# Three bank pairs in the up phases and a rearranged first up phase of a two-block fp32r transformer kernel

## The chip, the cores and the metric

The kernel runs on one core of one Trainium2 chip. The metric is the device time of one execution in microseconds (us); lower is better. PE is TensorE (PEld its weight loads), DVE is VectorE, ACT is ScalarE, POOL is GpSimd, and SP is SyncE, which issues most transfers. The text calls a matmul instruction a product.

## The reference

The input x has 256 rows of width 1024. Two transformer blocks follow each other. Cut to what matters here:

```python
# block 1
x = x + _moba(_rmsnorm(x, norm_mix), moba_w_qkv, moba_w_o)
u = _causal_dwconv(_rmsnorm(x, norm_ffn) @ w_up, conv_w, conv_b)   # D_FF = 2816, 3 taps
gate, up = jnp.split(u, 2, axis=-1)
x = x + (jax.nn.silu(gate) * up) @ w_down
x = _rmsnorm(x, norm_final)
# block 2: mod = silu(c) @ w_mod + b_mod gives shifts, scales and gates
x = x + 0.5 * (1 + ga1) * swiglu(modulate(rms_norm(x, g_ffn1), sh1, sc1), w1_gate, w1_up, w1_down)
x = x + (1 + ga2) * hybrid_mixer(modulate(rms_norm(x, g_mix), sh2, sc2), w_in, b_f, g_q, g_k, w_o)
x = x + 0.5 * (1 + ga3) * swiglu(modulate(rms_norm(x, g_ffn2), sh3, sc3), w2_gate, w2_up, w2_down)
```

All weights are float32.

## The kernel before

**Numbers in two parts.** Every weight and every activation that PE multiplies is split into a high part (rounded to fp32r, written by ACT) and a low part (the rest, a subtraction on DVE). One product of the reference is then three on PE: high by high (L1305), high weight by low activation (L1306), low weight by high activation (L1307).

**Slabs and chunks.** The weights come as slabs of 256 columns by up to 8 k-tiles (1 MB). SP loads slab i into one of three buffers `raw`; for each pair of k-tiles (a chunk) ACT writes `whi` (L688) and DVE writes `wlo` (L931), each in one of three buffers. The load of slab i + 3 waits for the last `wlo` of slab i.

**Phases.** Ten phases follow each other: qkv1, o1, up1, down1, up2, down2, qkv3, o3, up4, down4. up1 is the convolved FFN of block 1; up2 and up4 are the two gated ones of block 2. An up phase has 22 slabs and 22 groups, gate and up columns in turn; a group is the 256 output columns that PE accumulates in two banks of PSUM before somebody takes them out (evicts them). A slab of an up phase is 8 k-tiles x 2 halves x 3 = 48 products. A down phase has 4 groups of three slabs each (8, 8 and 6 k-tiles). The groups are numbered through the program: up1 has 16 to 37, down1 38 to 41, up2 42 to 63, down2 64 to 67, up4 85 to 106, down4 107 to 110.

**Banks.** Group g uses banks 2*(g%2) and 2*(g%2)+1, so two pairs in turn (`at`, L531 to L533). Before its first product PE waits until group g - 2 is evicted (`emptied(need, g - 2)`, L1296). Banks 4 (norm sums), 6 (transposes) and 7 are kept for other work; 4, 5, 1 and 3 also hold attention scores.

**Evictions.** In up1 (tags `cg`, `cu`) ACT scales the group and adds the bias into `ca` (L808), DVE adds the two other taps straight from the banks (L1079, four instructions; the last one frees the banks), then ACT applies silu for a gate group (L814), and for an up group DVE multiplies (L1091), ACT writes `Hhi` (L842, L847) and DVE `Hlo` (L1175). In up2 and up4 ACT's silu reads the gate group (L822) and DVE's multiplication the up group (L1113). The first groups of up2 and up4 take their norm afterwards and need more DVE work (L1103 to L1130).

**Order.** `Plan.lay` writes one list of steps, and each engine runs its own steps of it in that order: a step that waits holds up all later ones of its engine. `evict` puts weight conversions between the parts of an eviction. `MOD_STEPS` says at which slab a step `mod` is put: one dot product of `w_mod` on DVE (L1020), 72 in all. At the end of o1 the steps are the norm of up1 (PE sums the squares, L1318 and L1322; ACT takes the root, L745 and L748), then for each of 8 tiles `latey` (DVE L971 into `yb`, ACT L766 into the high part of `A`) and `latelo` (DVE L978, the low part). ACT needs one table of functions for ln and exp and another for silu; `silu()` loads the second (L673) and `exp_ln()` the first (L667).

**Resets.** At the start of some slabs (`RESETS`) PE issues one tiny product on constants (L1299), which in this trace also marks where a slab begins.

Of the kernel before, what the change touches and what calls it, by code (L numbers as in the profile page):

```python
# [14 lines left out]
P = 128  # L15
S = 256
# [4 lines left out]
C = 256  # L21
# [16 lines left out]
RAW_OF = {"up2": 0, "qkv3": 1, "up4": 2}  # L38
LATE_OF = {"up1": 0, "up2": 1, "qkv3": 2, "up4": 3}
S_BANKS = (4, 5, 1, 3)  # L40
HALVES = ("qkv1", "o1", "qkv3", "o3")
NORM_BANK, T_BANK, O_BANK = 4, 6, 7
O_BANKS = {2 * C: S_BANKS[0], 3 * C: S_BANKS[1]}
NORM_OF = {"qkv1": 0, "up1": 1, "up2": 2, "qkv3": 3, "up4": 4}
# [4 lines left out]
def slab_table(a):  # L49
# [38 lines left out]

RESETS = {"up1": (1, 6, 12, 18), "down1": (0,), "up2": (1, 4, 6, 14), "down2": (0,), "up4": (1, 4, 6, 14), "down4": (0,)}
MOD_STEPS = {  # L90
    "qkv1": lambda i: int(i > 2) + int(i in (4, 7, 10)), "o1": lambda i: int(i < 15), "up1": lambda i: int(i in (29, 33)),
    "down1": lambda i: int(i < 50), "up2": lambda i: int(i >= 55) * (1 + int(i % 4 == 3)), "down2": lambda i: int(i < 83),
    "qkv3": lambda i: int(i in (89, 91, 93, 95)), "o3": lambda i: 0, "up4": lambda i: int(i > 106) * int(i % 2 == 0), "down4": lambda i: 0}
QKV3_TILE = {0: 0, 512: 8, 1024: 16, 1536: 4, 2048: 12, 2560: 20}

# [21 lines left out]
class Plan:  # L117
# [13 lines left out]
    def lay(self):  # L131
        slabs, st = self.slabs, self.st
# [118 lines left out]
        norm = "qkv1"  # L251
# [46 lines left out]
        for i, (ph, tag, c0, k0, nk, last, width, _) in enumerate(slabs):  # L298
# [11 lines left out]
            g = o_group + c0 // C if tag == "o" else group  # L310
            if tag == "ot":
                g = o_group + 2
# [7 lines left out]
            for kt in range(nk):  # L320
                kg = k0 + (kt // 3 if tag == "ot" else kt)
# [53 lines left out]
            if i + 1 < len(slabs) and slabs[i + 1][0] != ph and ph in NEXT_NORM:  # L375
                norm = NEXT_NORM[ph]
                if norm == "up1":
                    st.put("norm", norm)
                    for n in range(KD):
                        st.put("latey", norm, n)  # L380
                        for m in ([n - 1] if n else []) + ([n] if n == KD - 1 else []):
                            st.put("latelo", norm, m)
# [14 lines left out]
def build_program(nc, a, out):  # L397
    with ExitStack() as ctx:  # L398
# [3 lines left out]
        def sem(name):  # L402
            return ctx.enter_context(nc.semaphore(name))

        banks = [ctx.enter_context(nc.psum_tensor(f"bank{i}", [P, 512], F32)) for i in range(8)]
# [7 lines left out]
        Ahi, Alo = A[:, :, 0, :], A[:, :, 1, :]  # L413
# [14 lines left out]
        meanf = sb("meanf", [P, P])  # L428
# [35 lines left out]
        plan = Plan(slabs)  # L464
        st, nth, heads, groups = plan.st, plan.st.nth, plan.heads, plan.groups
# [10 lines left out]
        s_ahi, s_alo, s_ashift = sem("s_ahi"), sem("s_alo"), sem("s_ashift")  # L476
# [45 lines left out]
        def halved(g):  # L522

            return groups[g][0] in HALVES and g not in unnormed

        def at(g, i, c0=0, c1=S):

            if groups[g][1] == "o" and groups[g][2] >= 2 * C:
                return banks[O_BANKS[groups[g][2]]][:, i * S + c0:i * S + c1]
            if halved(g):  # L530
                return banks[2 * (g % 2)][:, i * S + c0:i * S + c1]  # L531
            return banks[2 * (g % 2) + i][:, c0:c1]

        def head_bank(n):

            return banks[S_BANKS[n % 4]]

# [6 lines left out]
        def emptied(need, g):  # L544

            if g in by_silu:
                need.wait_ge(s_silu, 2 * silu_g[g])
            elif g >= 0:
                need.wait_ge(s_evicted, nth_evicted[g])
# [110 lines left out]
        def _(act):  # L660
            need = Once(act)
# [88 lines left out]
            def norm(ph):  # L750
                b = banks[NORM_BANK]
                exp_ln()
                need.wait_ge(s_eps, 2)
                need.wait_ge(s_sums, NORMS.index(ph) + 1)
                if ph == "up2":
                    root(Rr[:, 0, :], b[:, S:2 * S], 1)
                    root(Rr[:, 1, :], b[:, 0:S], 0)
                else:
                    root(Rr[:, 0, :], b[:, 0:S], 0)
                if ph in ("up1", "up2", "up4"):  # L760
                    silu()

            def late_hi(ph, n):
# [499 lines left out]
        def _(pe):  # L1263
            need = Once(pe)

            def here(tag, ph, kg, g):

                if tag in ("o", "ot"):
                    need.wait_ge(s_olo, (0 if ph == "o1" else 8) + kg + 1)
                    return Ohi[:, kg, :], Olo[:, kg, :], S  # L1270
                if tag == "down":
                    need.wait_ge(s_hlo, KF * FFN_OF[ph] + kg + 1)
                    return Hhi[:, kg, :], Hlo[:, kg, :], S
                if g in unnormed:
                    need.wait_ge(s_alo, 8 * NORM_OF[ph] + kg + 1)
                    need.wait_ge(s_ashift, SHIFTED[ph])
                    return Bhi[:, kg, :], Blo[:, kg, :], SA
                if ph in RAW_OF:
                    need.wait_ge(s_nlo, 8 * RAW_OF[ph] + kg + 1)
                else:  # L1280
                    need.wait_ge(s_alo, 8 * NORM_OF[ph] + kg + 1)
                return Ahi[:, kg, :], Alo[:, kg, :], S

            def multiply(i, kt):
                ph, tag, c0, k0, nk, last, width, _ = slabs[i]
                g = plan.group_of[i]
                kg = k0 + kt
                final = last and kt == nk - 1
                if tag == "ot":
                    g, kg, final = g - 2 + kt % 3, k0 + kt // 3, kt > 2  # L1290
                need.wait_ge(s_wlo, nth("lo", i, kt // 2))
                xh, xl, ncol = here(tag, ph, kg, g)
                if kg == 0 and tag == "o" and c0 >= 2 * C:
                    need.wait_ge(s_exp, soft[(12 if ph == "o1" else 28) + c0 // C - 2])
                elif kg == 0:
                    emptied(need, g - 2)  # L1296
                slab = i - plan.first_of[ph]
                if kt == 0 and slab in RESETS.get(ph, ()):
                    pe.matmul(banks[NORM_BANK][:, 511:512], meanf[:, :], meanf[:, 0:1], start=True, stop=True)  # L1299
                for j in range(1 if tag == "f" else 2):  # L1300
                    m = 104 if tag == "f" else P
                    hi = whi[:, i % SPL, kt, j * P:j * P + m]
                    lo = wlo[:, i % SPL, kt, j * P:j * P + m]
                    o = at(g, j, 0, ncol)[0:m, :]
                    pe.matmul(o, hi, xh, start=kg == 0 and not (j and halved(g)), stop=False)  # L1305
                    pe.matmul(o, hi, xl, start=False, stop=False)  # L1306
                    ins = pe.matmul(o, lo, xh, start=False, stop=final and (j == 1 or not halved(g)))  # L1307
                if kt % 2 == 1:
                    ins.then_inc(s_chunk, 1)

            def norm(ph):
                b = banks[NORM_BANK]
# [100 lines left out]
            def qk_norm(base):  # L1413
# [2 lines left out]
                pe.matmul(banks[T_BANK][:, :], blk[:, :], tmp[:, 0:2, :].rearrange("p a b -> p (a b)"), start=True,  # L1416
                          stop=True).then_inc(s_tpe, 1)

            part_of = {"mm": multiply, "norm": norm, "scores": scores, "turn": turn, "later": later,
                       "values": values, "vturn": v_turn, "qkn": qk_norm}  # L1420
            for step in st.list:
                if step[0] in part_of:
# [39 lines left out]
```

## Time and profile before

| what | value |
|---|---|
| device time, median of 3 runs | 831.17 us |
| the three runs | 829.16, 831.6, 831.17 us |
| the profiled execution: device time | 829.95 us |
| its span | 827.7 us |
| PE busy | 801.8 us (97%) |
| DVE busy | 644.9 us (78%) |
| ACT busy | 488.5 us (59%) |

The page's busy shares say that PE works nearly all of the time; the 2.25 us between the span and the execution's own time lie around the program. Matmuls overlap each other in the records (a duration of 276 ns where the next one starts 113 ns later), so the distance from start to start tells PE's pace, and the number in square brackets behind a row tells the idle time ahead of it and who ended it. A row that begins with a stretch A:B gives, in this order, its length, then for PE, PEld, DVE, ACT and POOL the busy time with the number of instructions, then PEclk (the clock granted to PE, where 1.00 is 2.4 GHz and 0.50 is 1.2 GHz), the busy share of the DMA engines and the GB/s they moved.

### The profile page before, as it was taken

The page shows a single profiled execution, that of the slowest core. Times are in us where ns is not written, and L with a number is a line of the kernel's source. Part 1 is how long each engine was busy: PE and PEld are TensorE (multiplying, and loading weights), DVE is VectorE, ACT ScalarE, POOL GpSimd, SP SyncE. Part 2 cuts the span into 40 slices and gives each one's busy share as a digit, 9 for nine tenths or more (in the row PEclk, how much of TensorE's full clock was granted, in tenths as well). Part 3 has the DMA queues.
Part 4 walks back from the last instruction along what each step waited for, and adds up shares of the span by engine and source line. Part 5 has one row for each costly group of instructions (what it writes and reads, how often), then busy time and mean ns, then how long its engine had stood idle before and what let it go on. Part 6 is the DMA issues. An engine that isn't in the chain of part 4 may idle for free. (4 is left out here: it accounts for less than half of the span.)

```text
span 827.7 us, 16827 instructions
## 1 busy us (share of the span) xinstructions
PE 801.8 (97%) x6818; PEld 779.6 (94%) x6818; DVE 644.9 (78%) x1331; ACT 488.5 (59%) x1015; POOL 21.1 (3%) x53
## 2 busy tenths in 40 slices
PE   6999997999999999999999999799999999999998
PEld 5899997999999999999999999789889999999998
DVE  5788877889899887999888887868657897765651
ACT  6755556766767565755555556665656765555440
POOL 1000000000000000000000000600000000000000
PEclk9999999999999999999999999999999999999999
DMA  8776673765565987499998876446343677665540
GB/s 287 257 233 233 200 245 118 242 202 191 196 224 172 325 298 253 152 304 334 348 321 296 295 252 213 131 128 192 106 137 103 204 234 255 224 204 192 191 154 27
DMA packets 150014, 179.44 MB, mean 217 GB/s; under 512 B 5681, under 2 KB 139569, under 8 KB 149937
## 3 DMA queue, kind: packets, MB, share of 16 engines
q1 hardware_dynamic: 148624, 178.17, 65.6%
q8 instruction: 54, 0.88, 0.4%
q0 software_dynamic: 1024, 0.03, 0.1%
q10 hardware_dynamic: 288, 0.16, 0.1%
q14 instruction: 24, 0.19, 0.1%
HBM read 177.27 MB, written 1.05 MB: 215 GB/s over the span
## 5 line engine op out<-in xcount | busy, mean ns | idle before, releaser
L931 DVE TENSOR_TENSOR wlo<-raw,whi 128x512 fp32r<-128x512 f32 x528 | 343.3, 685 | 69.1 <-ACT whi L688 68.4
L1305 PE MATMUL bank<-A,whi 128*128 128x256 f32 x1280 | 363.9, 284 | 12.3 <-DVE wlo L931 7.5
L688 ACT ACTIVATE whi<-raw 128x512 fp32r<-128x512 f32 x528 | 308.3, 622 | 100.2 <-PE bank L1307 94.5
L1306 PE MATMUL bank<-A,whi 128*128 128x256 f32 x1280 | 356.8, 279 | 0.0
L1307 PE MATMUL bank<-A,wlo 128*128 128x256 f32 x1280 | 356.7, 279 | 0.0
L1305 PEld LDWEIGHTS bank<-A,whi 128*128 128x128 f32 x1280 | 243.0, 190 | 15.6 <-DVE wlo L931 9.0
L1306 PEld LDWEIGHTS bank<-A,whi 128*128 128x128 f32 x1280 | 243.0, 190 | 1.0 <-issue 1.0
L1307 PEld LDWEIGHTS bank<-A,wlo 128*128 128x128 f32 x1280 | 243.0, 190 | 0.0
L1305 PE MATMUL bank<-Hhi,whi 128*128 128x256 f32 x528 | 146.0, 276 | 0.0
L1306 PE MATMUL bank<-Hlo,whi 128*128 128x256 f32 x528 | 145.7, 276 | 0.0
L1307 PE MATMUL bank<-Hhi,wlo 128*128 128x256 f32 x528 | 145.7, 276 | 0.0
L1306 PEld LDWEIGHTS bank<-Hlo,whi 128*128 128x128 f32 x528 | 99.1, 188 | 0.0
L1305 PEld LDWEIGHTS bank<-Hhi,whi 128*128 128x128 f32 x528 | 99.1, 188 | 0.0
L1307 PEld LDWEIGHTS bank<-Hhi,wlo 128*128 128x128 f32 x528 | 99.1, 188 | 0.0
L1020 DVE SCALAR_TENSOR_TENSOR mring<-mring,cact 128x1024 f32<-128x1024 f32 x72 | 87.2, 1220 | 0.0
L842 ACT ACTIVATE Hhi<-hb 128x256 fp32r<-128x256 f32 x33 | 13.8, 419 | 61.2 <-DVE hb L1113 35.6
L1305 PE MATMUL bank<-B,whi 128*128 128x258 f32 (+1 forms) x168 | 48.3, 287 | 1.1 <-DVE B L937 1.1
L1306 PE MATMUL bank<-B,whi 128*128 128x258 f32 (+1 forms) x168 | 47.7, 284 | 0.0
L1307 PE MATMUL bank<-B,wlo 128*128 128x258 f32 (+1 forms) x168 | 47.3, 281 | 0.0
L1079 DVE SCALAR_TENSOR_TENSOR ca<-bank,cols,ca 128x255 f32<-128x255 f32 (+1 forms) x88 | 36.5, 476 | 2.2 <-ACT ca L808 1.6
L1305 PE MATMUL bank<-Ohi,whi 128*128 128x256 f32 x128 | 37.0, 289 | 0.8 <-DVE wlo L931 0.8
L1307 PE MATMUL bank<-Ohi,wlo 128*128 128x256 f32 x128 | 35.7, 279 | 0.0
(148 smaller groups left out, 784.2 us busy)
## 6 DMA issues: line engine op xcount, KB each, us to landing
mring<-in_w_mod SPq DMA_DIRECT2D x72, 512.0 KB, 6.0
raw<-in_ffn_w_up SPq DMA_DIRECT2D x22, 1024.0 KB, 5.1
raw<-in_w_gate SPq DMA_DIRECT2D x22, 1024.0 KB, 5.4
raw<-in_w_up SPq DMA_DIRECT2D x22, 1024.0 KB, 5.8
raw<-in_w_down SPq DMA_DIRECT2D x16, 1024.0 KB, 5.4
raw<-in_w_in SPq DMA_DIRECT2D x12, 1024.0 KB, 5.4
raw<-in_moba_w_qkv SPq DMA_DIRECT2D x11, 1024.0 KB, 5.7
raw<-in_ffn_w_down SPq DMA_DIRECT2D x8, 1024.0 KB, 6.3
```

Of the source, the lines that this page charges most:

```text
L688: act.activation(whi[:, i % SPL, k0:k1, 0:width], raw[:, i % RAW, k0:k1, 0:width], ACT.Copy).then_inc(s_whi, 1)
L842: act.activation(Hhi[:, n, :], hb[:, 0, :], ACT.Copy).then_inc(s_hhi, 1)
L931: dve.tensor_tensor(lo, raw[:, i % RAW, k0:k1, 0:width], hi.bitcast(F32), ALU.subtract).then_inc(s_wlo, 1)
L1020: dve.scalar_tensor_tensor(out=w, in0=w, scalar=1.0, in1=cact[:, :], op0=ALU.mult, op1=ALU.mult, accum_out=msum[:, u:u + 1]).then_inc(s_ms ...
L1079: ins = dve.scalar_tensor_tensor(out=y[:, part:S], in0=at(g, i, 0, S - part), scalar=cvec[:, 2 - part, c:c + 1], in1=y[:, part:S], op0=ALU ...
L1305: pe.matmul(o, hi, xh, start=kg == 0 and not (j and halved(g)), stop=False)
L1306: pe.matmul(o, hi, xl, start=False, stop=False)
L1307: ins = pe.matmul(o, lo, xh, start=False, stop=final and (j == 1 or not halved(g)))
```

## The change

It makes these edits:

- In up1, up2 and up4 group number n of the phase uses pair n % 3 of the pairs (0, 1), (2, 3), (5, 6) (`UP_PAIRS`, `pair_of`). Other phases keep their banks. Before its first product a group now waits for the last earlier user of each of its banks (`users_before`) in place of group g - 2.
- The table of silu is no longer loaded behind up1's norm; it is loaded by the first silu of up1.
- In the first slab of up1 the product of the high parts waits for the high part of `A` only, and the low part is waited for ahead of the second product.
- Behind up1's norm, ahead of its first slab, PE makes nine 128x128 products of constants into bank 6 (`warm`).
- The `mod` step at slab 29 (in up1) is dropped and one at slab 50 (the last of down1) is added.

```diff
+THREE, UP_PAIRS = ("up1", "up2", "up4"), ((0, 1), (2, 3), (5, 6))
...
-    "qkv1": lambda i: int(i > 2) + int(i in (4, 7, 10)), "o1": lambda i: int(i < 15), "up1": lambda i: int(i in (29, 33)),
-    "down1": lambda i: int(i < 50), "up2": lambda i: int(i >= 55) * (1 + int(i % 4 == 3)), "down2": lambda i: int(i < 83),
+    "qkv1": lambda i: int(i > 2) + int(i in (4, 7, 10)), "o1": lambda i: int(i < 15), "up1": lambda i: int(i == 33),
+    "down1": lambda i: int(i < 51), "up2": lambda i: int(i >= 55) * (1 + int(i % 4 == 3)), "down2": lambda i: int(i < 83),
...
                 if norm == "up1":
                     st.put("norm", norm)
+                    st.put("warm")
...
+            if groups[g][0] in THREE:
+                return banks[pair_of(g)[i]][:, c0:c1]
             if halved(g):
                 return banks[2 * (g % 2)][:, i * S + c0:i * S + c1]
             return banks[2 * (g % 2) + i][:, c0:c1]
+
+        def pair_of(g):
+
+            return UP_PAIRS[(g - plan.group_of[plan.first_of[groups[g][0]]]) % 3]
+
+        def banks_of(g):
+            if groups[g][1] == "o" and groups[g][2] >= 2 * C:
+                return (O_BANKS[groups[g][2]],)
+            if groups[g][0] in THREE:
+                return pair_of(g)
+            return (2 * (g % 2),) if halved(g) else (2 * (g % 2), 2 * (g % 2) + 1)
+
+        def users_before(g):
+
+            return [max((h for h in range(g) if b in banks_of(h)), default=-1) for b in banks_of(g)]
...
-                if ph in ("up1", "up2", "up4"):
+                if ph in ("up2", "up4"):
                     silu()
...
-            def here(tag, ph, kg, g):
-
+            def here(tag, ph, kg, g, high=False):
+
+                if high:
+                    need.wait_ge(s_ahi, 8 * NORM_OF[ph] + kg + 1)
+                    return Ahi[:, kg, :], Alo[:, kg, :], S
...
-                xh, xl, ncol = here(tag, ph, kg, g)
+                early = i == plan.first_of["up1"]
+                xh, xl, ncol = here(tag, ph, kg, g, early)
...
                 elif kg == 0:
-                    emptied(need, g - 2)
+                    for before in users_before(g):
+                        emptied(need, before)
...
                     pe.matmul(o, hi, xh, start=kg == 0 and not (j and halved(g)), stop=False)
+                    if early:
+                        here(tag, ph, kg, g)
                     pe.matmul(o, hi, xl, start=False, stop=False)
...
+            def warm():
+
+                for _ in range(9):
+                    pe.matmul(banks[T_BANK][:, 0:P], meanf[:, :], meanf[:, :], start=True, stop=True)
```

**PE, from the norm of up1 to its first slab, before.** `acc` and `sq` are squares, `meanf` is a constant, `A` the normed activation.

```order
L1322 MATMUL bank<-sq,meanf 128x256 [waits s_sq]
L1322 MATMUL bank<-sq,meanf 128x256
L1305 MATMUL bank<-A,whi 128x256 [waits s_evicted,s_alo,s_wlo]
L1306 MATMUL bank<-A,whi 128x256
L1307 MATMUL bank<-A,wlo 128x256
```

The same place with the change:

```order
L1353 MATMUL bank<-sq,meanf 128x256 [waits s_sq]
L1353 MATMUL bank<-sq,meanf 128x256
L1340 MATMUL bank<-meanf 128x128 x9
L1329 MATMUL bank<-A,whi 128x256 [waits s_evicted,s_ahi,s_wlo]
L1332 MATMUL bank<-A,whi 128x256 [waits s_alo]
L1333 MATMUL bank<-A,wlo 128x256
```

The nine products stand ahead of the first slab, and the wait for the low part (s_alo) has moved from the first product to the second.

**ACT, behind the same norm, before** (L748 ends the root, L766 writes the high part of `A`):

```order
L745 ACTIVATE lnb<-bank,epsc 128x256 [waits s_root,s_sums]
L748 ACTIVATE Rr<-lnb 128x256 [waits s_ln]
L673 ACT_TABLE_LOAD
L766 ACTIVATE A<-yb 128x256 [waits s_latey] x8
L688 ACTIVATE whi<-raw 128x512 [waits s_chunk,s_raw0]
```

With the change the table load stands in the eviction of up1's first group:

```order
L827 ACTIVATE ca<-bank,cols 128x256
L707 ACTIVATE whi<-raw 128x512 [waits s_raw1]
L707 ACTIVATE whi<-raw 128x512 x2
L692 ACT_TABLE_LOAD [waits s_evicted]
L833 ACTIVATE ca<-ca 128x256 x2
L707 ACTIVATE whi<-raw 128x512
```

The load now waits for that group's eviction by DVE, and a weight conversion is queued behind it.

**PE, where down1 passes from its first group (38) to its second (39), before:**

```order
L1307 MATMUL bank<-Hhi,wlo 128x256
L1305 MATMUL bank<-Hhi,whi 128x256 [waits s_evicted,s_wlo]
L1306 MATMUL bank<-Hlo,whi 128x256
```

and with the change:

```order
L1333 MATMUL bank<-Hhi,wlo 128x256
L1329 MATMUL bank<-Hhi,whi 128x256 [waits s_wlo]
L1332 MATMUL bank<-Hlo,whi 128x256
```

The second group of down1 has no wait for an eviction of its own any more. A wait is left out only where an earlier one of the same semaphore already covered it.

## Rows read from the trace of the kernel before

**Rows 1.** Busy time by stretch: up1, then down1.
```profile
134.30:258.40 124.10, 123.25 (x1065) 122.94 (x1066) 112.62 (x234) 84.70 (x182) 0.00 (x0) 0.99 0.61 199
258.40:318.40 60.00, 60.00 (x532) 60.00 (x531) 51.94 (x97) 36.90 (x68) 0.00 (x0) 1.00 0.86 293
```

**Rows 2.** Timeline, start of up1 (start, duration, engine, line, tiles, count, idle before).
```profile
132.11 1.28 ACT L673 ACT_TABLE_LOAD   x1
132.12 0.88 DVE L971 SCALAR_TENSOR_TENSOR yb<-XT,cols,Rr 128x256 f32<-128x256 f32 x2 [2.62 <-ACT Rr L748]
133.85 0.42 DVE L978 TENSOR_TENSOR A<-yb,A 128x256 fp32r<-128x256 f32 x1 [0.85 <-ACT A L766]
134.37 0.36 PE L1305 MATMUL bank<-A,whi 128*128 128x256 f32 x1 [3.24 <-issue]
139.15 1.29 DVE L931 TENSOR_TENSOR wlo<-raw,whi 128x512 fp32r<-128x512 f32 x2
...
141.55 0.28 PE L1299 MATMUL bank<-meanf 128*128 128x1 f32 x2
```

**Rows 3.** Busy time by stretch around the two long pauses of PE: PEclk is third last.
```profile
135.50:138.80 3.30, 3.30 (x18) 3.30 (x17) 3.16 (x9) 2.04 (x6) 0.00 (x0) 0.50 0.00 0
...
523.60:527.60 4.00, 0.00 (x0) 0.00 (x0) 3.82 (x10) 3.62 (x7) 3.96 (x8) 1.00 0.17 21
528.00:531.40 3.40, 3.40 (x20) 3.01 (x17) 2.03 (x4) 1.88 (x4) 3.40 (x8) 0.50 1.05 293
```

**Rows 4.** Timeline of PE: the four waits for a bank in up1, up2 and up4.
```profile
158.71 0.36 PE L1305 MATMUL bank<-A,whi 128*128 128x256 f32 x1 [0.45 <-DVE ca L1079]
236.31 0.35 PE L1299 MATMUL bank<-meanf 128*128 128x1 f32 x2 [0.33 <-DVE ca L1079]
344.06 0.35 PE L1299 MATMUL bank<-meanf 128*128 128x1 f32 x2 [0.40 <-DVE bcol L1106]
...
669.93 0.28 PE L1307 MATMUL bank<-A,wlo 128*128 128x256 f32 x1
671.02 0.36 PE L1305 MATMUL bank<-A,whi 128*128 128x256 f32 x1 [0.81 <-DVE hb L1130]
```

**Rows 5.** Timeline of DVE in the middle of up1.
```profile
194.15 1.65 DVE L1079 SCALAR_TENSOR_TENSOR ca<-bank,cols,ca 128x255 f32<-128x255 f32 x4 [0.18 <-ACT ca L808]
...
202.80 1.90 DVE L931 TENSOR_TENSOR wlo<-raw,whi 128x512 fp32r<-128x512 f32 x3 [0.71 <-ACT whi L688]
204.88 1.65 DVE L1079 SCALAR_TENSOR_TENSOR ca<-bank,cols,ca 128x255 f32<-128x255 f32 x4 [0.18 <-ACT ca L808]
...
209.36 1.22 DVE L1020 SCALAR_TENSOR_TENSOR mring<-mring,cact 128x1024 f32<-128x1024 f32 x1
```

**Rows 6.** Timeline: the first silu of up1, and the next stop for a load.
```profile
144.71 2.09 DVE L931 TENSOR_TENSOR wlo<-raw,whi 128x512 fp32r<-128x512 f32 x3
144.83 0.72 ACT L814 ACTIVATE ca<-ca 128x256 f32<-128x256 f32 x2 [0.50 <-DVE ca L1079]
145.46 1.14 ACT L688 ACTIVATE whi<-raw 128x512 fp32r<-128x512 f32 x2
...
154.68 1.68 ACT L688 ACTIVATE whi<-raw 128x512 fp32r<-128x512 f32 x3 [1.14 <-DMA raw<-in_ffn_w_up]
155.35 1.29 DVE L931 TENSOR_TENSOR wlo<-raw,whi 128x512 fp32r<-128x512 f32 x2 [0.82 <-ACT whi L688]
```

**Rows 7.** Timeline, from up1 into down1 (L1299 at 258.39 is down1's first instruction).
```profile
258.39 0.28 PE L1299 MATMUL bank<-meanf 128*128 128x1 f32 x2
...
259.85 1.00 ACT L808 ACTIVATE ca<-bank,cols 128x256 f32<-128x256 f32 x2
...
260.50 1.65 DVE L1079 SCALAR_TENSOR_TENSOR ca<-bank,cols,ca 128x255 f32<-128x255 f32 x4 [0.27 <-ACT ca L808]
```

**Rows 8.** Timeline, from up2 into down2 (L1299 at 443.42 is down2's first instruction).
```profile
443.42 0.28 PE L1299 MATMUL bank<-meanf 128*128 128x1 f32 x2
443.62 0.76 DVE L1113 TENSOR_TENSOR hb<-bank,ca 128x256 f32<-128x256 f32 x2 [1.55 <-PE bank L1307]
```

More of the change, by code:

```diff
@@ L1417, in qk_norm @@
                           stop=True).then_inc(s_tpe, 1)
-            part_of = {"mm": multiply, "norm": norm, "scores": scores, "turn": turn, "later": later,
+            part_of = {"warm": warm, "mm": multiply, "norm": norm, "scores": scores, "turn": turn, "later": later,
                        "values": values, "vturn": v_turn, "qkn": qk_norm}
```

## The prediction

> **What bounds the kernel now.** I read the busy shares of the page first: PE works 97% of the span, so only what PE waits for, or runs slowly through, can be won. Then the waits by engine: around the three up phases PE stops once at the start of up1 and four times for a bank. Then the busy time by stretch: up1 and down1 are PE's, yet in up1 DVE is busy for 112.62 of 124.10 us as well [rows 1]. Then the timeline around each place that the change touches. Three things are to be seen there.
>
> First, ahead of up1 PE stands 3.24 us [rows 2], and the clock answers: PE works again from 134.37, and PEclk is 0.50 from 135.5 to 138.8 [rows 3]. The same follows a pause of 4 us in qkv3: 0.50 from 528.0 to 531.4 [rows 3]. A phase that PE bounds loses half of such a stretch, 3.4 / 2 = 1.7 us.
>
> Second, DVE and ACT run in a lockstep of their own in up1: the same eviction comes at 194.15 and 204.88, so 10.73 us for a pair of slabs, with DVE stopped inside it by ACT (0.71 and 0.18 us) and not by PE [rows 5]. PE's pace is 60.00 us for 532 instructions of down1 [rows 1], 0.113 each, or 10.8 us for the 96 products of a pair. So DVE hardly makes up what it has fallen behind, and nothing that brings PE forward brings DVE forward.
>
> Third, the last eviction of up1 is late. PE is done with group 37 at 258.39, ACT takes it up at 259.85, and DVE's last instruction on its banks ends at 260.50 + 1.65 = 262.15 [rows 7]. Nobody waits for that before, since group 38 needs only group 36.
>
> **The change part by part, worked against the profiled execution (829.95 us).**
>
> *Start of up1.* The table load of 1.28 us stands ahead of the high part of `A` [rows 2]. It begins together with DVE's first `yb`, 132.11 and 132.12; two of those take 0.88 us [rows 2], one about half a us. The high part needs the first `yb` anyway, so the chain comes forward by 1.28 - 0.52 = 0.76 us, not by 1.28. The wait for high parts alone lets one product start some 0.4 us earlier still (a low part takes 0.42 us [rows 2]), but the next one waits for the low part. The nine products of constants are some 18 passes, at 0.113 about 2.0 us, and should end about when the first high part is there. They fill the pause, so the fall of the clock at 135.5 goes. Then PE meets the next wait: the fourth `wlo` of the first slab is DVE's first instruction behind the low parts. It starts at 139.15 and takes half of 1.29 [rows 2], so it ends near 139.8 before and 139.05 now. Two k-tiles, 12 products = 1.4 us, come behind it, and the slab ends near 140.5 in place of 141.55 [rows 2]. PE gains 1.05 us.
>
> *Bank waits in up1.* 0.45 and 0.33 us idle [rows 4]. A stop costs 0.17 us more than its idle time: 1.09 us from start to start with 0.81 idle [rows 4], where 0.11 is the pace. Both go, since group g now waits for g - 3, a slab (5.4 us) older. PE's products of up1 end at 258.39 - 1.05 - 0.62 - 0.50 = 256.2.
>
> *Up1 into down1.* Group 37 is the 22nd of its phase, 21 % 3 = 0, so it uses banks 0 and 1. Group 38 is even and uses them too. `users_before` makes it wait for group 37, which PE has only just finished; that group 39 has lost its wait says the same. So down1 starts when DVE has evicted group 37, at 262.15 before. The `mod` step taken out of up1 gives 1.22 us [rows 5]. The start gives 0.76, but the table load now stands ahead of the first silu: the conversions behind it move from 145.46 by -0.76 + 1.28 = +0.52, and DVE's third `L931` of the row beside it waits for them [rows 6]. Ten us on, ACT stops 1.14 us for a load and DVE 0.82 behind it [rows 6]; a shift of +0.52 disappears in the 0.82. If the load lands when it did, the net shift is 0. Bounds: -0.31 if it lands sooner (0.52 - 0.82), +0.52 if it lands later by as much as it is asked for later. The eviction ends at 262.15 - 1.22 = 260.93. PE starts 0.10 behind the DVE instruction it waits for (134.37 behind 133.85 + 0.42 [rows 2]), so at 261.03 in place of 258.39: **+2.64 us**, a pause of 4.8 us for PE. All that the start of up1 and its bank waits gave lies inside that pause and is worth nothing.
>
> *The clock at down1.* 4.8 us is longer than both pauses that cost the clock [rows 2, 3]. Down1 is all PE's, 60.00 of 60.00 us [rows 1], so I take **+1.70**. Bounds: 0 if the clock stays, 3.4 if it stays low for two such stretches.
>
> *Up2 and up4.* Their bank waits go: 0.40 + 0.17 = **-0.57** and 0.81 + 0.17 = **-0.98** [rows 4]. The group that is now waited for is one slab older. Nothing else of PE's stops near either; at worst both terms are 0.
>
> *Up2 into down2.* Group 63 uses banks 0 and 1 again, and group 64 is even. It waits for L1113, done at 443.62 + 0.76 = 444.38 [rows 8], plus 0.10, in place of 443.42: **+1.06**. One us leaves the clock alone: the stops of rows 4 are of that size and nothing follows them. Up4 into down4 costs nothing: group 107 is odd, banks 2 and 3, last used two slabs before.
>
> *The `mod` step in down1.* 1.22 us more of DVE, where it has 60.00 - 51.94 = 8 us idle [rows 1], ahead of the last group's eviction, for which it waits on PE. Nothing; without that cover at most 1.22.
>
> Sum: 2.64 + 1.70 - 0.57 + 1.06 - 0.98 = **+3.85 us**, 833.8 for this execution. The median of the three timed ones is 1.2 us above it (831.17); the mean of all four is 830.5, and I give 830.5 + 3.85 = **834.3**. That is slower by 0.5%, where a measurement of this kernel can tell about 0.3% (2.5 us) from no change.
>
> **A rule against the rows, twice.** The table load takes 1.28 us and is followed by the high part of `A` without a gap: DVE gets its answer 0.46 us behind the load's end, one conversion later [rows 2]. The Trainium skill (ScalarE: Activation LUTs, "What ACT_TABLE_LOAD costs") has the same load with a drain of about 1.38 us. By it the conversions behind the first silu would be that much later again; the trace disagrees, and it is a rival only.
>
> The stops in rows 4 are stops for a bank, and each ends with the eviction named. The Trainium skill (TensorE: Matmul & The Clock Gate, "HAM oscillation — how this bites in real kernels") tells of a kernel in which double buffering in PSUM gave no further gain. By it the two gains would be nothing; this is the last rival.
>
> **The rivals.**
>
> *The clock holds.* The pause comes, its 1.70 does not: +2.15, 832.6. Against it: both long pauses of the trace were followed by 0.50 [rows 3]. Chance 0.13.
>
> *No pause at down1: faster.* If the third pair lets the evictions of up1 follow PE after all, group 37 is evicted right behind its last product, as group 63 is [rows 8]. Down1 starts at 256.2, -2.19, and with the other terms -2.68: 827.8. The sign turns where down1 starts at 258.9 (a pause too short for the clock), an eviction 2.6 us behind the last product. For it: before, it comes 3.8 us behind, not far from that. Against it: a period of 10.73 us with no stop for PE [rows 5]. Chance 0.08, and 0.06 for a pause in between, near no change.
>
> *ACT is shut for longer than the load.* If it is shut for as long again, 1.28 us, DVE's shift behind the 0.82 is 0.52 + 1.28 - 0.82 = +0.98: +4.8, 835.3. Against it: the row. Chance 0.06.
>
> *The third pair gives nothing.* PE's next wait in up2 and up4 (`wlo`, or silu) ends where the bank's did: +5.4, 835.9. Against it: a weight chunk is made two slabs ahead. Chance 0.07.
>
> **How the numbers follow.** The forecast keeps 0.60. Its own range, with a DVE shift of -0.31 to +0.52 and a clock price of 1.0 to 3.4, is 833.3 to 836.5. Down to 831.2 the range takes in the held clock and most pauses in between, up to 837.0 the last two rivals. Slower: 0.57 of the forecast, 0.12 of the last two, 0.01 of the first: 0.70. Faster: 0.08. Within 0.3%: 0.22.
>
> **What would show it.** Right: a stop of 4 to 5.5 us ahead of down1's first instruction, ended by the DVE line that evicts up1's groups, and PEclk 0.50 behind it for 3.4 us; no 0.50 behind the start of up1, where PE stops about 1 us for the fourth `wlo`; a stop near 1 us at down2; none of the four bank waits; DVE's period in up1 still 10.7 us. Wrong: a short stop at down1, a shorter period, or PEclk 1.00 behind the pause.

## The result, and the profile after

| | before | changed |
|---|---|---|
| median (8 runs each, side by side) | 831.38 us | 835.42 us |
| lowest to highest | 829.16 to 834.36 us | 833.78 to 836.93 us |
| profiled execution, device time | 829.95 us | 836.44 us |
| its span | 827.7 us | 834.2 us |

The ratio is 1.0051, with a 95% interval from 1.0034 to 1.0069: slower by 0.5%, 4.0 us. 834.3 had been forecast.

The page of the changed kernel, its first part (busy time, share of the span, instructions):

```profile
PE 807.0 (97%) x6836; PEld 785.1 (94%) x6836; DVE 645.4 (77%) x1331; ACT 489.0 (59%) x1015; POOL 21.1 (3%) x53
```

The shares read as before. The waits of PE in the changed kernel, longest first (line, what it waited for, us in total, times, longest), show what changed:

```profile
PE bank L1329 <- DVE wlo L950: 9.5, 3, 7.7
PE bank L1323 <- DVE ca L1098: 4.3, 1, 4.3
PE bank L1374 <- DVE QKV L1084: 4.1, 1, 4.1
PE bank L1329 <- DVE B L956: 1.3, 1, 1.3
PE bank L1323 <- DVE hb L1132: 0.9, 1, 0.9
```

The four waits of [rows 4] are gone. In their place stand the second row (4.3 us, the reset product that opens down1, for L1098, DVE's eviction of up1's groups) and the fifth (0.9 us, the reset that opens down2).

Timeline of the changed kernel, start of up1, its first silu, and DVE in the middle of up1:

```profile
131.04 2.17 PE L1340 MATMUL bank<-meanf 128*128 128x128 f32 x18
...
133.23 0.35 PE L1329 MATMUL bank<-A,whi 128*128 128x256 f32 x1
...
138.47 1.29 DVE L950 TENSOR_TENSOR wlo<-raw,whi 128x512 fp32r<-128x512 f32 x2
139.21 0.39 PE L1329 MATMUL bank<-A,whi 128*128 128x256 f32 x1 [1.05 <-DVE wlo L950]
...
143.96 1.28 ACT L692 ACT_TABLE_LOAD   x1 [0.49 <-DVE ca L1098]
145.25 0.72 ACT L833 ACTIVATE ca<-ca 128x256 f32<-128x256 f32 x2
145.88 2.18 ACT L707 ACTIVATE whi<-raw 128x512 fp32r<-128x512 f32 x4
...
153.65 2.50 DVE L950 TENSOR_TENSOR wlo<-raw,whi 128x512 fp32r<-128x512 f32 x4
153.87 1.66 ACT L707 ACTIVATE whi<-raw 128x512 fp32r<-128x512 f32 x3
...
193.32 1.65 DVE L1098 SCALAR_TENSOR_TENSOR ca<-bank,cols,ca 128x255 f32<-128x255 f32 x4 [0.18 <-ACT ca L827]
204.05 1.65 DVE L1098 SCALAR_TENSOR_TENSOR ca<-bank,cols,ca 128x255 f32<-128x255 f32 x4 [0.19 <-ACT ca L827]
```

The products of constants (each is two passes, hence x18) end at 133.21, and the first slab starts 0.02 behind them, 1.14 us before that of [rows 2]. It stops once, 1.05 us, for the fourth `wlo`. The table load has moved to 143.96, and the next activation starts 0.01 us behind its end. At 153.65 and 153.87 neither DVE nor ACT stops for the load that stopped them for 0.82 and 1.14 us in [rows 6]. And L1098 still comes back after 204.05 - 193.32 = 10.73 us, the period of [rows 5].

Timeline of the changed kernel, from up1 into down1, and from up2 into down2:

```profile
255.72 0.28 PE L1333 MATMUL bank<-A,wlo 128*128 128x256 f32 x1
...
257.88 1.00 ACT L827 ACTIVATE ca<-bank,cols 128x256 f32<-128x256 f32 x2
258.52 1.65 DVE L1098 SCALAR_TENSOR_TENSOR ca<-bank,cols,ca 128x255 f32<-128x255 f32 x4 [0.27 <-ACT ca L827]
260.32 0.56 PE L1323 MATMUL bank<-meanf 128*128 128x1 f32 x2 [4.32 <-DVE ca L1098]
...
449.05 0.28 PE L1333 MATMUL bank<-A,wlo 128*128 128x256 f32 x1
449.36 0.76 DVE L1132 TENSOR_TENSOR hb<-bank,ca 128x256 f32<-128x256 f32 x2 [1.55 <-PE bank L1333]
450.26 0.35 PE L1323 MATMUL bank<-meanf 128*128 128x1 f32 x2 [0.94 <-DVE hb L1132]
```

PE starts its last product of up1 at 255.72 and then waits 4.32 us for an eviction that ends at 260.17; the next phase follows 0.15 us behind. Against [rows 7] down1 starts 1.93 us later, although PE's last product of up1 starts 2.55 us earlier (258.27 before).

Busy time by stretch of the changed kernel: just behind that stop, the start of up1, all of down1, its middle, the middle of down2, and the first 16 us of up2's second part (PEclk is third last):

```profile
260.40:266.20 5.80, 5.80 (x27) 5.80 (x28) 4.78 (x13) 2.12 (x5) 0.00 (x0) 0.50 0.46 144
133.30:138.00 4.70, 4.64 (x36) 4.39 (x36) 4.68 (x13) 2.64 (x7) 0.00 (x0) 1.00 0.00 0
260.40:325.40 65.00, 65.00 (x530) 65.00 (x531) 50.73 (x93) 35.55 (x63) 0.00 (x0) 0.96 0.78 263
270.00:310.00 40.00, 40.00 (x342) 40.00 (x341) 31.22 (x55) 22.68 (x39) 0.00 (x0) 1.00 0.79 267
455.00:495.00 40.00, 40.00 (x355) 40.00 (x354) 32.10 (x56) 22.29 (x37) 0.00 (x0) 1.00 0.86 280
350.70:366.70 16.00, 16.00 (x144) 16.00 (x143) 15.73 (x34) 9.38 (x20) 0.00 (x0) 1.00 0.70 233
```

The same view of the kernel before for the last three of these:

```profile
270.00:310.00 40.00, 40.00 (x355) 40.00 (x355) 34.65 (x63) 25.09 (x46) 0.00 (x0) 1.00 0.91 313
455.00:495.00 40.00, 40.00 (x356) 40.00 (x355) 33.30 (x61) 22.33 (x40) 0.00 (x0) 1.00 0.81 270
344.30:360.30 16.00, 15.99 (x136) 15.81 (x137) 15.73 (x33) 9.14 (x20) 0.00 (x0) 1.00 0.70 234
```

Three things are to be seen. Behind the stop PEclk is 0.50 for the whole first row: 27 products in 5.8 us. Down1 as a whole takes 65.0 us for 530 products, where [rows 1] has 60.0 for 532. And of these 5 us the clock explains only a part: in the middle of down1, with PEclk at 1.00, PE makes 342 products in 40 us where it made 355, so one takes 117 ns and not 113. Down2 of the same execution keeps 355. I call this pace the slow rhythm. It costs 13 products in 355, over some 59 us 2.2 us. The records name it: a product of the slow rhythm is recorded with 281 ns, one of the usual pace with 276.

### The profile page after: what moved, and what is told of

It reads as the page before. It is cut to its first block, busy times and chain, and to the rows that moved or that the text cites. A ratio compares the mean times of both kernels' runs of the same rounds, so it can differ in the third digit from the quotient of the medians.

```text
span 834.2 us, 16859 instructions
## 1 busy us (share of the span) xinstructions
PE 807.0 (97%) x6836; PEld 785.1 (94%) x6836; DVE 645.4 (77%) x1331; ACT 489.0 (59%) x1015; POOL 21.1 (3%) x53
## 3 DMA queue, kind: packets, MB, share of 16 engines
HBM read 177.27 MB, written 1.05 MB: 214 GB/s over the span
## 4 chain that ended last, share of the span: by engine, by line
PE 85%; DVE 6%; ACT 6%; issue 2%; DMA 1%; SPq 0%; DVEq 0%; ACTq 0%
PE bank L1329 26%; PE bank L1333 26%; PE bank L1332 26%; ACT whi L707 1%; PE bank L1430 1%; DVE wlo L950 1%; PE bank L1381 1%; DMA raw<-in_moba_w_qkv 1%; PE bank L1397 1%; DVE yb L990 1%; PE bank L1374 1%; ACT sq L748 0%; PE bank L1349 0%; PE bank L1447 0%; PE bank L1441 0%
## 5 line engine op out<-in xcount | busy, mean ns | idle before, releaser
L1329 PE MATMUL bank<-Hhi,whi 128*128 128x256 f32 x528 | 148.1, 281 | 0.0
L1332 PE MATMUL bank<-Hlo,whi 128*128 128x256 f32 x528 | 147.7, 280 | 0.0
L1333 PE MATMUL bank<-Hhi,wlo 128*128 128x256 f32 x528 | 147.7, 280 | 0.0
L1332 PEld LDWEIGHTS bank<-Hlo,whi 128*128 128x128 f32 x528 | 101.1, 191 | 0.0
L1098 DVE SCALAR_TENSOR_TENSOR ca<-bank,cols,ca 128x255 f32<-128x255 f32 (+1 forms) x88 | 36.6, 476 | 2.0 <-ACT ca L827 2.0
L1332 PE MATMUL bank<-Olo,whi 128*128 128x256 f32 x128 | 35.6, 278 | 0.0
```

What stands on the lines that cost most here:

```text
L1098: ins = dve.scalar_tensor_tensor(out=y[:, part:S], in0=at(g, i, 0, S - part), scalar=cvec[:, 2 - part, c:c + 1], in1=y[:, part:S], op0=ALU ...
```

## The experiments

Each ratio is against the kernel before, run beside it. The medians of before in the three sets were 830.38, 830.49 and 829.91 us (17 to 19 runs each).

### The pairs alone, and the rest alone

The theory: the loss is the collision of banks 0 and 1 at the ends of up1 and up2, and the rest of the change is worth about what the earlier start is. `e_banks_only` is the kernel before with

```diff
+THREE, UP_PAIRS = ("up1", "up2", "up4"), ((0, 1), (2, 3), (5, 6))
```

and its waits; the table, the early product, the constants and the `mod` steps stay as before.

> The kernel before with the three pairs of banks alone (table load, waits, constants' products and mod steps as before). Theory (DVE and ACT set the end of up1): the last eviction of up1 ends where it did before, 262.15 us, so down1 starts at 262.3, 3.9 us later than before; with the half clock behind it, 1.1 at down2 and -0.6 and -1.0 in up2 and up4 this gives 5.1 to 6.8 us over the kernel before, 836.5 to 838.2: the slowest of all. Rival (evictions follow PE once banks are free): last eviction of up1 earlier by the bank waits, 1.1 us or more, and a time of 835 or less.

Measured: 836.61 us (836.02 to 837.23), ratio 1.0079 [1.0063, 1.0094]. Its timeline, up1 into down1:

```profile
260.36 1.65 DVE L1097 SCALAR_TENSOR_TENSOR ca<-bank,cols,ca 128x255 f32<-128x255 f32 x4 [0.27 <-ACT ca L826]
262.16 0.56 PE L1322 MATMUL bank<-meanf 128*128 128x1 f32 x2 [5.36 <-DVE ca L1097]
```

The eviction ends at 262.01, against 262.15 in [rows 7]: two bank waits less for PE, and DVE is hardly earlier (0.14 us). That is the core of the forecast, that DVE sets the end of up1.

`e_start_only` is the changed kernel with two pairs again:

```diff
-THREE, UP_PAIRS = ("up1", "up2", "up4"), ((0, 1), (2, 3), (5, 6))
+THREE, UP_PAIRS = (), ((0, 1), (2, 3), (5, 6))
```

> The changed kernel with two pairs of banks as before (the four other edits stay). Theory: the 1.05 us won at the start of up1 are worth what the bank waits of up1 let through. DVE's evictions come 0.8 us earlier there, so the first bank wait (158.7 us before) ends near 157.9 and the second is gone with the dropped mod step: up1 ends 1.0 to 1.5 us earlier, no stop at down1 or down2, the waits of up2 and up4 stay: 829.9 to 830.4, that is 1.0 to 1.5 us under the kernel before. Rival (the start edits cost through the table load ahead of the first silu): equal to the kernel before or slower.

Measured: 829.20 us (827.89 to 829.87), ratio 0.9985 [0.9973, 0.9997]: 1.2 us under the kernel before. So the pairs cost 5 to 6 us and all else gives about one.

### The pairs in another order

If the collision is the cause, the same three pairs in an order that ends up1 and up2 on another pair should bring the gain without the stop. `e_turned` changes only that; the 22nd group (21 % 3 = 0) then uses banks 5 and 6:

```diff
+LATE_PAIRS, TURNED = ((5, 6), (0, 1), (2, 3)), ("up1", "up2")
...
-            return UP_PAIRS[(g - plan.group_of[plan.first_of[groups[g][0]]]) % 3]
+            pairs = LATE_PAIRS if groups[g][0] in TURNED else UP_PAIRS
+            return pairs[(g - plan.group_of[plan.first_of[groups[g][0]]]) % 3]
```

> The changed kernel with one edit: up1 and up2 take the three pairs in the order (5, 6), (0, 1), (2, 3), so that their last group lies in banks 5 and 6 and the first group of down1 and of down2 finds banks 0 and 1 used two slabs before. Theory (the stop ahead of down1 is the wait for the eviction of up1's last group): both stops are gone, down1 starts at about 256 us in the trace, no half clock follows there, and all that the edits save shows: 1.0 at the start, 1.1 of bank waits in up1, 0.6 in up2, 1.0 in up4, so about 3.7 us under the kernel before, 827.5. Rival (the third pair gives nothing, PE's next wait ends where the bank's did): stops of PE for wlo or silu in up1, up2 or up4, and a time within 1 us of the kernel before. Rival (the clock is the whole cost): stop at down1 remains.

Measured: 825.48 us (824.90 to 826.78), ratio 0.9948 [0.9932, 0.9963]. It beats the changed kernel by about 9 us and the kernel before by 4.9, where the expectation had 3.7. Its timeline at the same place, and then the middles of down1 and down2 by stretch:

```profile
255.92 0.28 PE L1335 MATMUL bank<-A,wlo 128*128 128x256 f32 x1
256.04 0.28 PE L1325 MATMUL bank<-meanf 128*128 128x1 f32 x2
256.18 0.36 PE L1331 MATMUL bank<-Hhi,whi 128*128 128x256 f32 x1
```

```profile
270.00:310.00 40.00, 40.00 (x356) 40.00 (x355) 35.03 (x65) 25.16 (x46) 0.00 (x0) 1.00 0.91 311
455.00:495.00 40.00, 40.00 (x356) 40.00 (x355) 32.25 (x59) 22.38 (x40) 0.00 (x0) 1.00 0.85 283
```

No stop: down1 starts 2.35 us earlier than in [rows 7], with PEclk at 1.00 behind it and 356 products in 40 us in both phases. The gains that the forecast saw inside the pause are real once the pause is gone, and larger than summed, because the slow rhythm is in the kernel before too. It stands behind two of the four bank waits of [rows 4]: from 158.9 to 169.9 and from 344.5 to 355.7, 94 products each with records of 281 ns. Each of the two stretches ends at the next reset product (170.09, 355.92). The groups of products of `before`, by line, from 345.0 to 355.5 and then from 356.5 to 366.0 (the last number ahead of the second bar is the mean in ns):

```profile
L1306 PE MATMUL bank<-A,whi 128*128 128x256 f32 x30 | 8.4, 281 | 0.0
L1306 PE MATMUL bank<-A,whi 128*128 128x256 f32 x29 | 8.0, 276 | 0.0
```

94 products at 118 ns in place of 113 are 0.4 us, so these two bank waits cost that much more than their stops.

`e_turned_up1` turns up1 alone (`TURNED = ("up1",)`), so the stop at down2 stays.

> The kernel with the turned order of pairs in up1 alone; up2 keeps (0, 1) first, so the first group of down2 still waits for up2's last eviction. Theory: 1.1 us slower than with both turned (825.5), about 826.6, with a stop of 0.9 to 1.0 us idle ahead of down2 and none ahead of down1. Rival (the stop at down2 is absorbed later): 825.5.

Measured: 827.34 us (826.86 to 829.16), ratio 0.9960 [0.9946, 0.9974]; the expectation was 826.6. The stop at down2 is there again (0.94 us idle), and in the profiled execution, at 829.16 the slowest of its eight, down2 ran in the slow rhythm:

```profile
455.00:495.00 40.00, 40.00 (x342) 40.00 (x341) 31.25 (x58) 21.74 (x39) 0.00 (x0) 1.00 0.81 264
```

So a stop of one us, behind which the clock does not fall, can be followed by the slow rhythm too.

### The stop filled with products

To tell the price of the clock from the price of the stop, `e_filled` puts 19 products of constants into bank 7 behind up1's last product, ahead of down1's first wait:

```diff
+            if ph == "down1" and first:
+                st.put("fillup")
...
+            def fillup():
+
+                for _ in range(19):
+                    pe.matmul(banks[O_BANK][:, 0:P], meanf[:, :], meanf[:, :], start=True, stop=True)
```

> The changed kernel with 19 products of constants (38 passes of 128 columns, some 4.1 us) into bank 7 ahead of the first wait of down1. The stop of down1 stays in time, down1 starts where it did (260.3 us), but PE is busy in it. Theory (4.6 us of stop, and on top of it a half clock of 1.7 to 3.4 us): PEclk stays at 1.00 behind down1's start and the kernel is faster than the changed one by 1.7 to 3.0 us, 832.4 to 833.7. Rival (the clock does not matter to the end, something else paces down1's first 6 us): the same time as the changed kernel, 835.4.

Measured: 834.73 us (832.89 to 836.77), ratio 1.0061 [1.0042, 1.0080]. Its timeline, and its busy time behind the start of down1 and in the middles of both down phases:

```profile
255.31 4.40 PE L1342 MATMUL bank<-meanf 128*128 128x128 f32 x38
259.81 0.35 PE L1325 MATMUL bank<-meanf 128*128 128x1 f32 x2
```

```profile
260.00:266.80 6.80, 6.80 (x59) 6.80 (x59) 6.05 (x16) 3.91 (x8) 0.00 (x0) 1.00 0.58 178
270.00:310.00 40.00, 40.00 (x342) 40.00 (x341) 30.75 (x56) 23.26 (x41) 0.00 (x0) 1.00 0.83 278
455.00:495.00 40.00, 40.00 (x356) 40.00 (x355) 32.13 (x58) 22.63 (x40) 0.00 (x0) 1.00 0.86 283
```

The clock holds, as meant, and yet the time is hardly better, above the 832.4 to 833.7 of the theory: down1 runs in the slow rhythm although PE had no pause. The run alone could not say what the clock costs, so I ran it again beside the changed kernel itself.

> The changed kernel with the stop of down1 filled by 19 products of constants, beside the changed kernel on one chip. Theory (half clock behind the stop costs on its own): 1.0 to 3.0 us faster than the changed kernel. Rival (the clock there costs nothing at the end): equal within 0.5 us. The first run of it was 834.7 us against 835.4 of the changed kernel on another chip, which does not tell the two apart.

> The changed kernel itself, on the same chip as the next three, so that the filled pause and the turned pairs can be compared with it directly. Both theories: 0.5% over the kernel before, with a stop of some 4.5 us ahead of down1 and half clock behind it.

Measured: 833.92 us (830.87 to 836.50, 12 runs), ratio 1.0030 [1.0011, 1.0050], for `e_filled_again`, and 834.84 us (832.89 to 835.35), ratio 1.0046 [1.0029, 1.0062], for `e_changed_again`. The twelve of the first fall into three heaps: five at 830.9 to 831.9, three at 833.8 to 834.3, four at 835.5 to 836.5. Both down phases of its profiled execution (835.54, in the highest heap) are slow, 342 products in 40 us each. None, one or two slow down phases, at 2.3 us each, would give such heaps; only one of the twelve has a profile, so that is argued, not shown. In `e_changed_again` down1 is fast and down2 slow, the reverse of the changed kernel's first profile:

```profile
270.00:310.00 40.00, 40.00 (x356) 40.00 (x355) 32.25 (x59) 23.54 (x42) 0.00 (x0) 1.00 0.81 279
455.00:495.00 40.00, 40.00 (x342) 40.00 (x341) 30.86 (x55) 21.16 (x36) 0.00 (x0) 1.00 0.81 268
```

### A second reset in the down phases

The reset products looked like the place where a rhythm could be changed: each down phase has one, at its first slab, right where the stop now stands. `e_resets` puts a second one a slab later, where PE has long been running, and `e_filled_resets` adds the filled stop.

```diff
-RESETS = {"up1": (1, 6, 12, 18), "down1": (0,), "up2": (1, 4, 6, 14), "down2": (0,), ...
+RESETS = {"up1": (1, 6, 12, 18), "down1": (0, 1), "up2": (1, 4, 6, 14), "down2": (0, 1), ...
```

> The changed kernel with one more reset product in down1 and one in down2, at their second slab. In the profiles so far a down phase that began behind a stop (or behind the filled stop) ran in 7 of 11 cases at 117.8 ns a product in place of 113.3 up to the next reset product, with PEclk at 1.00; of 9 down phases without a stop ahead none did. Theory (the stop can leave PE in a slower rhythm, a reset product ends it): at most the first slab of each phase is slow (0.2 us), no down phase takes over 60.2 us apart from half clock, and the median is 1.0 to 3.0 us under the changed kernel: 832 to 834, with less spread. Rival (the rhythm is settled anew at each reset by chance, or by something else in the down phases): 117.8 ns behind the second reset too in some phase, and the time of the changed kernel, 834.8.

> The same resets with the filled stop ahead of down1. Beside the kernel with the resets alone, the half clock is the only difference. Theory (half clock behind down1's stop costs 1.7 to 3.4 us on its own): 1.5 to 3 us faster than with the resets alone, about 831. Rival (the clock's price is no more than 0.5 us): equal.

Measured: 835.89 us (833.80 to 836.46), ratio 1.0061 [1.0041, 1.0082], where the reset theory had 832 to 834; and 833.78 us (831.13 to 835.53), ratio 1.0039 [1.0023, 1.0054], where about 831 was expected. Busy time by stretch, behind the start of down1, of `e_resets`:

```profile
261.30:265.30 4.00, 4.00 (x20) 4.00 (x20) 3.54 (x10) 1.99 (x5) 0.00 (x0) 0.50 0.32 113
```

and of `e_filled_resets`, with the middle of its down2:

```profile
260.70:264.70 4.00, 4.00 (x37) 4.00 (x37) 3.53 (x11) 2.65 (x6) 0.00 (x0) 1.00 0.39 139
455.00:495.00 40.00, 40.00 (x342) 40.00 (x341) 30.62 (x55) 21.94 (x38) 0.00 (x0) 1.00 0.83 274
```

The reset theory falls as it was put: in `e_filled_resets` the records of down2 are 281 ns on both sides of the second reset product (451.50), up to its end. But a reset product can end the slow rhythm. In down1 of `e_resets` the last 26 products ahead of the second reset product (268.82), behind the half clock, are slow and those behind it are not. Its groups of products by line, from 265.8 to 268.5 and from 269.5 to 279.0:

```profile
L1333 PE MATMUL bank<-Hhi,wlo 128*128 128x256 f32 x9 | 2.5, 281 | 0.0
L1333 PE MATMUL bank<-Hhi,wlo 128*128 128x256 f32 x29 | 8.0, 276 | 0.0
```

With the two stretches of `before` and one of `e_start_only` (343.0 to 354.2, reset product at 354.45), four of five long slow stretches of up1, up2 and the down phases that met a reset product ended there. Whether the reset product does it or the change of slab that comes with it, no run tells.

The pair also prices the clock, since the two differ only in the filled stop: 835.89 - 833.78 = 2.1 us, as far as the slow rhythm, which comes and goes, is equally frequent in both. The two traces agree. From the first to the last of its 528 products of data down1 takes 62.09 us in `e_resets` and 60.06 in `e_filled_resets`, 2.03 less, with only those 26 slow products (0.1 us) in the first.

### The other edits, one undone at a time in the turned kernel

These three start from `e_turned`, where no pause swallows what the start of up1 gives. `e_turned_nowarm` leaves the constants out:

```diff
-                    st.put("warm")
```

> Both phases turned, but without the nine products of constants ahead of up1. PE then pauses some 2.2 us there. Theory (they hold the clock): 0.50 follows in part of the executions; since PE has a spare us in the first slab anyway (it waits for the fourth wlo), the loss is 0.7 to 1.7 us where it falls: 826.2 to 827.2. Rival (2.2 us are too short a pause for the clock): no 0.50 there and 825.5, the nine products are worth nothing.

Measured: 826.20 us (825.19 to 826.94), ratio 0.9945 [0.9930, 0.9960]. Timeline and busy time at the start of up1:

```profile
133.22 0.35 PE L1330 MATMUL bank<-A,whi 128*128 128x256 f32 x1 [2.03 <-issue]
```

```profile
134.20:137.60 3.40, 3.40 (x18) 3.40 (x17) 3.40 (x11) 1.89 (x5) 0.00 (x0) 0.50 0.00 0
```

PE starts at 133.22 (`e_turned` at 133.42), and behind the 2.03 us idle its clock falls. Yet down1's first product of data starts at 255.98, no later than the 256.18 of `e_turned`: the first slab waits for the fourth `wlo` anyway, and the half clock falls inside that wait. Counted from the last product of up1's norm sums, the same point comes after 125.17 us here and after 125.16 in `e_turned`. The medians differ by 0.7 us, the ratios by 0.0003: I can't show that the constants are worth anything.

`e_turned_table` loads the table of silu behind up1's norm again:

```diff
-                if ph in ("up2", "up4"):
+                if ph in ("up1", "up2", "up4"):
```

> The kernel with the turned pairs, and the table of silu loaded behind the norm again as in the kernel before. Theory: the fourth wlo of up1's first slab comes 0.76 us later, and the slab ends that much later; PE's pause behind the constants' products grows to about 1.4 us, too short for the clock. 0.8 us slower than with turned pairs alone: 826.3. Rival (the load ahead of the first silu costs what it saves): equal, 825.5.

Measured: 825.98 us (825.67 to 827.31), ratio 0.9945 [0.9924, 0.9966]. The medians differ by 0.5 us, the ratios by 0.0003 the other way, so the times can't tell. The traces can: from the last product of up1's norm sums to down1's first product of data it is 125.96 us here and 125.16 in `e_turned`. The moved load is worth 0.80 us there, as expected (0.8).

`e_turned_mod` puts the `mod` steps back to where they were before.

```diff
-    ... "up1": lambda i: int(i == 33),
-    "down1": lambda i: int(i < 51), ...
+    ... "up1": lambda i: int(i in (29, 33)),
+    "down1": lambda i: int(i < 50), ...
```

> The kernel with the turned pairs, and the mod steps where the kernel before has them (slab 29, none at slab 50). DVE's evictions in the second half of up1 come 1.2 us later. Theory (with three pairs that end in banks 5 and 6 an eviction has a slab more of room): no stop of PE anywhere in up1 or at down1, equal to the turned kernel, 825.5 within 0.5. Rival (evictions lag by more than the room): a stop at the end of up1 and 826.5 or more.

Measured: 825.66 us (825.04 to 826.19), ratio 0.9938 [0.9917, 0.9959]: the time of `e_turned`, and by the same count in the traces 125.20 us for 125.16. A `mod` step less for DVE in up1 pays only where PE waits for DVE at its end, as in the changed kernel.

## Why the prediction was right, and which sizes were off

*Start of up1.* As forecast: the clock holds, PE stops once for the fourth `wlo` (1.05 us). The first slab ended at 140.69 where 140.5 had been written, so the start gave 0.86 for the 1.05. The next product behind up1 could have started at 255.8, where 256.2 had been written: the bank wait at 158.71 was worth its 0.62 and the slow rhythm behind it, 0.4 more.

*Bank waits in up1, up2 and up4.* All four are gone. For up4 the forecast was -0.98; that phase took 1.09 less. For up2 it was -0.57, and here the size was off. From down1's last product to down2's first product of data it is 125.2 us before and 125.1 after, though the latter has a new stop of 1.1, and 123.9 in `e_turned`, which has none: up2 itself gained 1.3. The rows show where most of the other 0.7 is: behind the stop at 344.06 of [rows 4] PE made 136 products in 16 us with PEclk at 1.00, and 144 in the same piece now. 94 of the 136 are in the slow rhythm, 0.4 us; the rest stays open. The prediction had it that nothing follows stops of this size. That holds for the clock; the slow rhythm followed two of the four.

*Up1 into down1.* The mechanism is the forecast's, with +1.93 in place of +2.64. The step that failed is the net shift of DVE, taken as 0 with bounds of -0.31 to +0.52. The conversions behind the first silu did move, from 145.46 [rows 6] to 145.88: +0.42 for the +0.52 forecast. What was wrong is what disappears behind them. I let the missing stop win back DVE's own 0.82 at most. But that DVE stop waits for ACT, and ACT's own stop for the load had been 1.14 [rows 6]; in the changed kernel the load is there in time and neither stops. Reckoned with ACT's 1.14 the shift is 0.42 - 1.14 = -0.72, and the eviction at up1's end came at 260.17 in place of 260.93, -0.76. That the load came in time because it was asked for sooner I did not test.

*The clock at down1.* It fell, as forecast. The size is not one number. In the first profile it was 0.50 from 259.4 to 266.2, of which 5.9 us fell on down1's products: 2.96 us. In `e_changed_again` it was 0.50 for 3.4 us, 1.7 us, which is the value forecast. `e_resets` against `e_filled_resets` gives 2.1 us over eight and twelve executions. All lie between the bounds of 0 and 3.4. The length of down1, from the first to the last of its 528 products of data, keeps clock and rhythm apart: 59.81 us before, 61.43 with 3.4 us of half clock alone (`e_changed_again`), 62.15 with the slow rhythm alone (`e_filled`), 64.62 with both (the changed kernel's first profile).

*Up2 into down2.* +1.06 forecast, 1.1 measured (0.94 idle, 1.21 from start to start with 0.11 as the pace).

*The `mod` step in down1.* Nothing, as forecast; `e_turned_mod` shows no gain of both `mod` edits together without the stop.

*What had no term.* The slow rhythm, 2.3 us for a whole down phase (62.15 - 59.81), in about one of the two phases. With the measured sizes the sum would be about 3.85 - 0.7 (down1's start) - 0.7 (up2) - 0.1 (up4) + 0.4 (the clock) + 2.3 (the rhythm) = +5. Measured were +4.0 and, in `e_changed_again`, +4.35, each with an interval of some 1.4 us either way. The direction came from the mechanism; that the figure is so near comes partly from misses that cancel.

The profiled pair adds up. From the first product of data of one phase to that of the next, down1 began 2.2 us late (260.74 for 258.53), took 4.8 us more, up2 0.1 less with its stop, down2 the same, qkv3 to the middle of up4 0.6 more (its half clock lasted 6.8 us instead of 3.4, and some came back), up4 1.1 less: +6.5, which is the span's 834.2 - 827.7. The profiled execution is the second slowest of its eight, and its mean granted clock (0.991) is at the low end of theirs (0.991 to 0.996): most others have less half clock. That they also have less of the slow rhythm is likely, but without their profiles not shown.

*The rivals.* "The clock holds", "no pause" and "a pause in between" fell by the rows of the changed kernel. "The third pair gives nothing" fell too: in `e_turned` its waits are gone and the time with them, 829.20 to 825.48 against `e_start_only`, which lacks only the pairs. The Trainium skill says of another kernel that double buffering in PSUM gave no further gain (TensorE: Matmul & The Clock Gate, "HAM oscillation — how this bites in real kernels"); that does not hold for this one, where each removed wait had been a stop of PE. "ACT shut for longer than the load" fell as well: the load at 143.96 takes 1.28 us and the next activation starts at 145.25. The Trainium skill (ScalarE: Activation LUTs, "What ACT_TABLE_LOAD costs") has a drain of about 1.38 us with the load; no row here shows time lost behind it.

## What to carry to other kernels

When buffers rotate with a new period, write down which buffer the last user of a phase has and which the first user of the next one wants: here a phase of 22 groups by three pairs ended on the pair that the next one opens with, and turning the order by one place made a loss of 4 us a gain of 5. A wait removed in a phase that another engine paces only gathers at the phase's end, so first ask whether the end lets it through. And a stop of PE ahead of a phase that PE bounds should be priced above its idle time, by the clock behind it and by the pace of the products that follow.

## What the runs showed of the hardware that was not expected

**A slower pace at full clock.** Of 15 down phases (down1 and down2) that a stop or the filled stop preceded, 8 ran at 342 products in 40 us, 117 to 118 ns each, with PEclk at 1.00. Of 13 that nothing preceded, none did; they made 355 or 356. One product's record is longer too, some 281 ns for 276. It was seen behind 1.2 us stops as well as behind 4.6 us ones, and in two of the three down phases behind a stop filled with products. It differs between executions of one kernel. In `before` it follows bank waits of 0.45 and 0.40 us idle in up1 and up2, for 94 products each. Four of five long stretches that met a reset product ended there, one went on; a down phase of this kernel has no reset product behind its start. DVE is not busier in it (31.2 us of 40 against 34.7 before). What it is stays open: no run here changed PE's operands, weight loads or banks in a down phase with a stop ahead of it.

**The half clock's length differs.** Behind the same stop it was 3.4 us in one execution and 6.8 in another, and behind qkv3's pause 3.4 before and 6.8 after. It also followed an idle time of 2.03 us in `e_turned_nowarm`, while the stops of 1.2 us from start to start at down2 were not followed by one.
